# Taking the seven groups of unused TensorE products out of a four-block transformer kernel

## What is computed

```
x -> block 0:  h = rms_norm(x) * (1 + sc1) + sh1          # sc, sh, g from c @ ada_w: 6 vectors a layer
               y = [mLSTM(h), MoBA attention(h)] @ w_out
               x = x + g1 * y
               h = rms_norm(x) * (1 + sc2) + sh2
               x = x + g2 * peer(h)
  -> block 1:  the same with differential attention in place of mLSTM and MoBA
  -> block 2:  x = x + [neighbourhood, dilated, memory attention](rms_norm(x)) @ w_out
               x = x + hierarchical_moe(rms_norm(x))        # 32 experts, top 2, silu(x w1) * (x w3) @ w2

peer(h): q = h @ wq; per token and head the 16 best of 128 x 128 experts by product keys;
         sum over 8 heads x 16 experts of  gate * gelu(u_e . h) * v_e
```

## Time and profile before

| what | us |
|---|---|
| median of 3 runs | 2945.67 |
| lowest and highest of them | 2941.66, 2954.51 |
| the profiled execution, its own time | 2953.61 |
| its span, first to last instruction | 2951.8 |
| PE busy in the span | 2330.9 (79%) |
| DVE busy | 1270.7 (43%) |
| ACT busy | 586.1 (20%) |
| POOL (GpSimd) busy | 592.1 (20%) |
| mean granted clock of PE, as a share of 2.4 GHz | 0.904 |
| DMA, mean over the span | 299 GB/s |

### The profile page before, as it was taken

How to read it: one execution, slowest core, us unless ns; L and a number is a source line. 1 busy time by engine, 2 the same in 40 slices (tenths; PEclk the granted TensorE clock), 3 DMA queues, 4 the chain that set the end, 5 groups by cost and what they waited for, 6 DMA issues and landing times.

```text
span 2951.8 us, 23183 instructions
## 1 busy us (share of the span) xinstructions
PE 2330.9 (79%) x7816; PEld 1129.6 (38%) x7816; DVE 1270.7 (43%) x3396; ACT 586.1 (20%) x1439; POOL 592.1 (20%) x564
## 2 busy tenths in 40 slices
PE   6976898877787778998887777777799996666666
PEld 2732246322232225564632322232375663222221
DVE  1032124777777753163477777675302423100110
ACT  1022211222222221131122222222112321000000
POOL 1000002544444440000254444444200000000000
PEclk8977799999999999959999999999899557888888
DMA  9432835999999995301599999999733013999998
GB/s 335 150 113 106 336 131 193 420 421 421 421 421 421 421 421 236 143 1 59 192 422 422 422 421 422 421 422 421 274 145 119 1 57 140 428 428 429 428 429 349
DMA packets 105035, 882.81 MB, mean 299 GB/s; under 512 B 16162, under 2 KB 16192, under 8 KB 19232
## 3 DMA queue, kind: packets, MB, share of 16 engines
q0 software_dynamic: 77264, 551.41, 45.5%
q1 hardware_dynamic: 27664, 330.08, 27.8%
HBM read 880.34 MB, written 6.06 MB: 300 GB/s over the span
## 4 chain that ended last, share of the span: by engine, by line
DMA 46%; PE 39%; DVE 7%; issue 4%; ACT 3%; SPq 0%; POOL 0%; DVEq 0%; POOLq 0%; ACTq 0%
DMA arena<-in_peer_uv_dram,arena 32%; DMA arena<-in_moe_pieces_dram 13%; PE gp L737 11%; PE gp L727 6%; PE summed L908 3%; PE scores L801 3%; PE turned L908 3%; PE summed L825 2%; PE gp L713 2%; PE turned L815 1%; PE gp L1040 1%; PE turned L759 1%; PE gp L723 1%; PE gp L724 1%; DMA arena<-in_w_slots_dram 1%
## 5 line engine op out<-in xcount | busy, mean ns | idle before, releaser
L1629 DVE CUSTOM_DVE_ANT_0 y<-arena,h 128x1024 f32<-128x1024 f32 x512 | 627.1, 1225 | 352.6 <-DMA arena<-in_peer_uv_dram,arena 337.1
L672 POOL DMA_INDIRECT arena<-in_peer_uv_dram,arena x512 | 563.5, 1101 | 829.5 <-PE summed L908 335.3
L908 PE MATMUL turned<-arena 128*128 128x512 f32 x1024 | 481.6, 615 | 157.2 <-ACT arena L1263 157.1
L908 PE MATMUL summed<-arena 128*128 128x512 f32 x1024 | 478.1, 613 | 148.8 <-ACT arena L1263 148.2
L908 PEld LDWEIGHTS turned<-arena 128*128 128x128 f32 x1024 | 188.0, 193 | 450.7 <-ACT arena L1263 260.1
L908 PEld LDWEIGHTS summed<-arena 128*128 128x128 f32 x1024 | 188.3, 193 | 437.2 <-ACT arena L1263 242.4
L737 PE MATMUL gp<-hT,arena 128*128 128x256 f32 x1408 | 314.4, 386 | 3.7 <-ACT hT L1157 2.7
L1263 ACT ACTIVATE arena<-cst,arena 128x128 f32<-128x128 f32 x512 | 177.5, 393 | 607.0 <-DVE arena L1646 604.2
L737 PEld LDWEIGHTS gp<-hT,arena 128*128 128x128 f32 x1408 | 271.9, 194 | 44.4 <-ACT hT L1157 4.3
L1040 PE MATMUL gp<-arena,mod 128*32 128x512 f32 x1024 | 165.3, 782 | 115.6 <-DMA arena<-in_moe_pieces_dram 114.4
L727 PE MATMUL gp<-arena,hT 128*128 128x512 f32 x416 | 182.4, 599 | 2.1 <-ACT hT L1157 2.1
(11 more groups left out here) (281 smaller groups left out, 1865.3 us busy)
## 6 DMA issues: line engine op xcount, KB each, us to landing
arena<-in_moe_pieces_dram SPq DMA_DIRECT2D x96, 2048.0 KB, 25.7
arena<-in_w_slots_dram SPq DMA_DIRECT2D x60, 2048.0 KB, 7.9
arena<-in_peer_uv_dram,arena POOLq DMA_INDIRECT x512, 21.3
t_rep<-t_rows POOLq DMA_DIRECT2D x1, 3066.0 KB, 13.1
arena<-t_rep POOLq DMA_DIRECT2D x1, 2304.0 KB, 27.9
na_rep<-na_rows POOLq DMA_DIRECT2D x1, 1778.0 KB, 11.6
mod<-na_rep POOLq DMA_DIRECT2D x16, 96.0 KB, 25.8
x<-in_x_dram SPq DMA_DIRECT2D x1, 1024.0 KB
```

The costliest lines, as they stand in the source:

```text
L672: pool.indirect_dma_start(rowbuf[b], None, a["peer_uv"].rearrange("l n d -> (l n) d"), bass.IndirectOffsetOnAxis(ap=idx[:, g:g + 1], axis= ...
L908: mm = pe.matmul(acc[:, n, :], diag[:, g % DIAGS, :], rowbuf[g % ROWS][:, D + n * 512:D + (n + 1) * 512], start=g % SLOTS == 0, stop=g % S ...
L1629: v.tensor_tensor_reduce(y[:, g % 2, :], rowbuf[g % ROWS][:, 0:D], h[:, u // PEER_H, :], 1.0, 0.0, ALU.mult, ALU.add, dots[:, g:g + 1]).th ...
```

## The change

All calls of `keep_clock` and the helper itself are taken out, with the wait that each call began with. Nothing else is edited.

```diff
-            def keep_clock(name, n):
-
-
-                pe.wait_ge(gemm_moved, last_group[name])
-                for _ in range(n):
-                    pe.matmul(gp[:, 0, :], ident, cst[:, 0:512], start=True, stop=True)
-
...
@@ head_sums
                     pe.matmul(norm_bank(b)[32 * j:32 * (j + 1), :], blk[:, 48:80], work[:, (i % 2) * 512:(i % 2) * 512 + 512],
                               start=True, stop=True).then_inc(qk_sum, 1)
-                keep_clock({"moba": "in0", "diff": "in1", "block2": "in2"}[stage_name], 3)
...
@@ mlstm
                 mm.then_inc(gates_t, 1)
-                keep_clock("in0", 4)
                 pe.wait_ge(silu_done, 8)
...
@@ the main line
             mm.then_inc(t5_mm, 1)
-            keep_clock("ada", 6)
             turn_h(0)
...
             for l in range(2):
-                keep_clock(f"out{l}", 15)
                 turn_h(2 * l + 1)
                 hT_ready()
                 peer(l)
                 peer_sum(l)
-                keep_clock(f"wq{l}", 13)
                 turn_h(2 * l + 2)
...
                     attention("diff")
-                    keep_clock("in1", 12)
                     pe.wait_ge(y_ready, 2)
...
             project("out2")
-            keep_clock("out2", 8)
             turn_h(6)
```

## The result

| | before | after |
|---|---|---|
| median, us | 2951.86 | 2960.53 |
| lowest and highest of 11 runs each, us | 2941.66, 2956.26 | 2955.81, 2967.92 |
| the profiled execution, us | 2953.61 | 2960.53 |
| its span, us | 2951.8 | 2958.7 |
| its mean granted clock | 0.904 | 0.887 |

The account below looks back on a forecast made before the run. It took DMA (46% of the chain) and PE (39%) as bounding the kernel. Terms 6.9 + 4.7 + 2.0 + 0.4 = 14.0 us, added to the median 2945.67, gave about 2960 us; 8 in 10 range 2947 to 2974.

Parts of the forecast that it names:

- The products lie beside waits; their 89 us free nothing: All removed groups: except at two head sums, PE still waits for another engine afterwards, so removing 89.1 us frees nothing.
- The four turns with a projection behind them, +6.9: After out0, wq0, in1 and out1: turns begin at 1.2 GHz and projections lose pace; +6.9 us net, bounds +1.5 to +9.4.
- The turn after `out2` and the router, +4.7: After the last output projection: turn +1.29 us, the router's 32 short products +3.4 us at the lower clock.
- the DMA-bound last stage starts later by all of it: Last stage: weight pieces are asked for as PE uses earlier ones, so the whole +4.7 us delay carries through.
- Nothing before them can raise the clock for long: Router after out2: no work ahead of its 32 products restores the clock, so +3.4 us, nearly the upper end of +4.1.
- The first head sums, +2.0: First attention: PE idles some 4.2 us, so the 16 spreading instructions run slower; +2.0 us, bounds 0 and +3.9.
- The second and third head sums, 0.2 each: Second and third attention: no gain, a new gap of about 2.7 us costs a little clock; bounds 0 and +2 each.
- The rest at nothing: After the first ada group, in the mLSTM and after wq1: removal costs nothing; if wrong, one turn, 1.3 us each.
- The sum, 14.0: Whole kernel: 6.9 + 4.7 + 2.0 + 0.4 = 14.0 us slower, with bounds of roughly +3 to +23.
- The pace of 7.19 us for 32 instructions: Full-clock pace used for one projection that took 9.22 us, giving a loss of 2.03 in the mean of 1.36.
- The first attention is entered slow: Rival, chance 0.13: clock stays down through four rounds before the wait at 286, adding 19 us, about 2979.
- Not slower, by a shift in the same stage: Rival, chance 0.13: three half-clock rounds behind the first attention's weight wait speed up, 14 us return, about 2946.

Follow-up runs that it names:

- transposes: Before with each unused product replaced by 7 transposes of a 128x128 block, of about the same PE time; 2960.84 us, ratio 1.0024.
- fill_all: Before with unused products added or increased at many places, including all three attentions and the turns; median 2925.93 us of six runs, 2885.69 to 2962.73.
- after_again: The kernel after timed once more, unchanged; 2963.20 us, ratio 1.0030 to before.
- idle_off: Before without only the products after the first ada group, in the mLSTM and after wq1; 2965.34 us, ratio 1.0056.
- entr_off: Before without only the products after out0, out1, wq0 and in1; 2964.58 us, ratio 1.0050.
- early_end: Before with fewer products after out0, out1, wq0, wq1, in1 and out2, so those groups end well ahead of the turn; 2969.03 us, ratio 1.0041.
- fill_wait_off: After with 8 unused products in the first attention, ahead of the wait for layer 1's weights; 2950.32 us, ratio 0.9996 to before.

## Why the prediction came out, point by point

- **The products lie beside waits; their 89 us free nothing.** Right. PE's busy time fell by 79.9 us and the time rose.
- **The four turns with a projection behind them, +6.9.** Right in mechanism, sized somewhat high. In the pair of profiles they give 3.2 + 0.6 + 2.7 - 0.1 = 6.4. Over twelve profiles (all but transposes and fill_all) the means with and without the groups differ by 2.26 (out0), 0.86 (wq0), 1.75 (in1) and 0.97 (out1), together 5.8. The weakest step is the turn after `out1`, where the working has about 2. With its group that turn still ran slow in three profiles of seven (5.13, 5.25, 5.29 us to the projection, against 4.09), and without it four of five took no longer (5.00 to 5.07; 5.62 in after_again).
- **The turn after `out2` and the router, +4.7.** After has 4.3 (11.50 against 7.24). The mean over the same twelve is lower, 2.9, because in three of five the clock rose inside the turn and the router took 5.0 and not 7.04. To the end of the program it is 4.0 by the means, so the step "the DMA-bound last stage starts later by all of it" held. "Nothing before them can raise the clock for long" was wrong: the 16 transposes can.
- **The first head sums, +2.0.** 2.3, shown in every profile that lacks them.
- **The second and third head sums, 0.2 each.** Undersized: 1.4 each. The working had the gap of 2.7 us and called its cost "a little clock". The row shows 2.64 us of idleness and then 3 us of work at 0.50. It lay within the bounds of 0 and 2.
- **The rest at nothing.** Right in the stage rows, but by its ratio idle_off is 0.56% above before. So "nothing" is not shown for the time, only for the rows.
- **The sum, 14.0.** The pair gives 15.7 in the priced places. By the means over profiles it is 5.8 + 2.9 + 2.3 + 2.8 = 13.8. Measured in time, by the ratios: 11 and 9 us.
- **Two readings in it are off, and neither moves the sum.** The pace of 7.19 us for 32 instructions stands in no row; 32 of that width take 7.07 at full clock at 2135.74 of the same profile, which makes that loss 2.15 and the mean 1.38. And the turn at 2411.94 does not stand behind a long wait but behind 0.51 us of idleness: it was slow because the third attention ahead of it ran at 0.50.
- **"The first attention is entered slow", chance 0.13.** It did not occur. The rounds between the spreading and the wait run at 1.92 us a slot in after, at full clock.
- **"Not slower, by a shift in the same stage", chance 0.13.** Half of this happened. Behind the wait, one round of after ran at 0.50 where before had three, as the working of this rival has it, and its first attention was 8.2 us shorter. It did not cancel the sum, since the block's output projection and norm behind it took 3.2 us longer and the other places cost their 15.7. The first forecast of this rival, that the place is unprotected and moves from run to run, was right, and the prediction gave it too little weight as a source of scatter.

The 2960.53 against 2960 forecast is partly luck, then. The forecast was carried from a median of 2945.67 of three runs, and 11 runs put before at 2951.86. The cost was forecast at 14 and is about 10; the start was 6 too low.

**What stays open.** idle_off, entr_off and early_end are slower than the priced places explain: by 14, about 9, and some 10 us. In which stage, the profiles taken cannot tell. Within one kernel the time of a run goes with its mean granted clock: before's runs beside idle_off range from 2922 us at 0.917 to 2963 at 0.899, and a line through all 30 gives some 20 us for each 0.01. Between kernels that mean says little, since it counts the waits too: fill_wait_off has 0.894 and idle_off 0.896, and fill_wait_off is 15 us faster. The first attention is the candidate: 126.01, 122.64 and 133.37 us in those three profiles, nearly all of it behind the wait for weights. But in entr_off and early_end the code up to its end is that of before, which took 118.34 and 113.94, so this is as well chance of single profiles. The part ahead of it moves as well: the first spreading begins between 257.2 and 263.6 us in the fourteen profiles, at 258.7 and 261.5 in the two of before. Whether and why the head sums' products and the stay at 0.50 behind that wait go together was not tried further.

## What to carry to other kernels

Unused products cost no time here while they filled a wait, and their worth is read at one point: the clock under the work right behind the wait. Count only groups that end just ahead of it, take their worth from a row at either clock, and expect it to differ from run to run. Before pricing entrances of 1 to 5 us, look at the mean clock of each long stage made of short products: one such stage at 0.61 held 20 us, more than four times any entrance, and four products were enough to get it. Another at 0.50, the third attention, was never freed in a profile. Where the same code gives 114 or 133 us from run to run, fix that stage first, or parts of a change will not add up.

## What the runs showed of the hardware

- The length of a wait does not by itself tell the clock behind it. Behind 2.64 us the next 3 us of work ran at 1.2 GHz (after, at 1253.67), and behind 2.21 us a turn took 4.00 us (before, at 1150.67); behind 2.49 us the turn after `out0` ran at 2.4 GHz, and behind 3.79 us the first eight transposes did (before, at 2146.60).
- Transposes alone held the clock at 1.00 for 10.4 us, and raised it inside a turn of 16 (0.74 over after's turn at 1391), though not in every such turn (0.50 over after's at 425).
- A stage of short products can stay at either clock for its whole length. The second attention ran 56.9 us at 0.98 or 78.7 at 0.61. The third ran 146 us at 0.50 with PE busy for 99% of it (fill_all), and 0.50 with 99% over 2295 to 2410 in before, so a full PE is no sign of a full clock.
- In the first attention the clock came back inside a modulation slot each time, after 1 to 5 whole rounds at 0.50 in six profiles whose code is the same up to there.
- Within one kernel the time of a run follows its mean clock, 2886 us at 0.940 to 2963 at 0.910 for one and the same kernel (fill_all).
